# Second block of a two-part network: gate folded into the output weights by GpSimd, norms applied per token out of PSUM, first expert item peeled

## The reference, cut to what matters

```python
h = rms_norm(x, g_mix) * (1.0 + sc1) + sh1
attn = sliding_window_sink_attention(q, k, v, sinks)             # 512 wide
lru  = rg_lru(xc, ...) * gelu(xg)                                # 512 wide
merged = concat([rms_norm(attn, g_attn_out), rms_norm(lru, g_lru_out)])
x = x + gt1 * (merged @ w_out)                                   # gt1: one row of 1024
h = rms_norm(x, g_ffn) * (1.0 + sc2) + sh2
# router: top 4 of 32 experts for each token, softmax over the 4
# expert: gu = h @ w_gu[e] + b_gu[e]; clamp; ((up + 1) * gate * sigmoid(1.702 gate)) @ w_down[e] + b_down[e]
x = x + gt2 * sum of the 4 experts, weighted
return rms_norm(x, g_final)
```

## Time and profile before

| | us |
|---|---|
| median of three runs (2158.57 to 2161.81) | 2161.07 |
| the profiled execution, its own time | 2167.19 |
| its span | 2165.3 |
| TensorE matmul busy | 2047.4 (95%) |
| VectorE / ScalarE / GpSimd busy | 598.2 / 308.1 / 61.6 |
| bytes moved | 598.74 MB, mean 277 GB/s |

### The profile page before, as it was taken

How to read it: one execution, slowest core, us unless ns; L and a number is a source line. 1 busy time by engine, 2 the same in 40 slices (tenths; PEclk the granted TensorE clock), 3 DMA queues, 4 the chain that set the end, 5 groups by cost and what they waited for, 6 DMA issues and landing times.

```text
span 2165.3 us, 24331 instructions
## 1 busy us (share of the span) xinstructions
PE 2047.4 (95%) x10023; PEld 1172.9 (54%) x10023; DVE 598.2 (28%) x1189; ACT 308.1 (14%) x695; POOL 61.6 (3%) x68
## 2 busy tenths in 40 slices
PE   8988999999998999999979999999999999999997
PEld 7766678847866778855735333333333333333332
DVE  0468443312267440003443111111111111111112
ACT  1324210000324310001321000000000000000001
POOL 0022000000012000000001000000000000000000
PEclk9979899999979999999988999999999999999999
DMA  7430068864422036444506999999999999999997
GB/s 301 155 117 1 1 257 301 342 256 156 156 78 79 1 137 228 151 168 155 207 5 272 383 429 427 429 428 429 427 429 428 429 428 428 429 428 429 429 428 298
DMA packets 44272, 598.74 MB, mean 277 GB/s; under 512 B 5056, under 2 KB 5360, under 8 KB 8464
## 3 DMA queue, kind: packets, MB, share of 16 engines
q1 hardware_dynamic: 44208, 597.82, 67.5%
HBM read 596.73 MB, written 1.07 MB: 276 GB/s over the span
## 4 chain that ended last, share of the span: by engine, by line
PE 76%; DMA 16%; DVE 6%; ACT 2%; issue 1%; SPq 0%; DVEq 0%; ACTq 0%
PE ps L1918 16%; DMA ring<-in_stream 16%; PE ps L1240 14%; PE ps L1261 7%; PE ps L1965 7%; PE ps L376 6%; PE ps L1892 3%; PE ps L390 2%; PE ps L1167 2%; PE ps L1907 2%; PE ps L1996 2%; PE ps L1635 2%; PE ps L1474 1%; PE ps L777 1%; PE ps L789 1%
## 5 line engine op out<-in xcount | busy, mean ns | idle before, releaser
L1918 PE MATMUL ps<-ring,HT 128*64 128x512 f32 x2176 | 481.3, 594 | 26.3 <-DMA ring<-in_stream 25.5
L1918 PEld LDWEIGHTS ps<-ring,HT 128*64 128x64 f32 x2176 | 151.9, 137 | 349.2 <-issue 284.8
L1240 PE MATMUL ps<-XT,ring 128*128 128x256 f32 (+1 forms) x1536 | 306.0, 362 | 3.3 <-DVE XT L313 3.3
L1240 PEld LDWEIGHTS ps<-XT,ring 128*128 128x128 f32 x1536 | 271.9, 190 | 36.8 <-DVE XT L313 3.7
L1965 PE MATMUL ps<-SB,HT 128*64 128x512 f32 x1088 | 250.9, 615 | 0.9 <-ACT HT L2021 0.9
L1965 PEld LDWEIGHTS ps<-SB,HT 128*64 128x64 f32 x1088 | 77.4, 141 | 171.6 <-issue 171.6
L1261 PE MATMUL ps<-ring,HT 128*128 128x512 f32 x352 | 151.7, 592 | 0.0
L2069 DVE TENSOR_SCALAR HT<-ps 128x512 f32<-128x512 f32 x34 | 23.5, 692 | 457.2 <-PE ps L1918 457.2
L2013 ACT ACTIVATE HT<-HT 128x512 f32<-128x512 f32 x34 | 21.4, 630 | 781.8 <-DVE HT L2069 781.8
L2081 DVE TENSOR_TENSOR HT<-ps,TOK 128x512 f32<-128x512 f32 x34 | 23.5, 692 | 376.9 <-PE ps L1965 376.9
L376 PE MATMUL ps<-XT,ring 128*128 128x256 f32 x576 | 126.4, 383 | 1.3 <-DMA ring<-in_stream 1.3
(11 more groups left out here) (411 smaller groups left out, 1801.1 us busy)
## 6 DMA issues: line engine op xcount, KB each, us to landing
ring<-in_stream SPq DMA_DIRECT2D x210, 2048.0 KB, 19.7
SB<-in_stream SPq DMA_DIRECT2D x68, 2048.0 KB, 19.8
SB<-in_ln SPq DMA_DIRECT2D x8, 512.0 KB, 9.5
CST<-in_const SPq DMA_DIRECT2D x1, 1362.0 KB, 5.5
PAR<-in_layer SPq DMA_DIRECT2D x2, 558.5 KB, 11.2
X<-in_x SPq DMA_DIRECT2D x1, 1024.0 KB, 5.0
HN<-in_head_norm SPq DMA_DIRECT2D x2, 512.0 KB, 12.0
SB<-mod_rows SPq DMA_DIRECT2D x2, 512.0 KB, 4.4
```

Source lines behind the costliest of these rows:

```text
L1240: m = pe.matmul(ps[:, 2 * (f % 2) + a, j * T + cols.start:j * T + cols.stop], w[:, k, a, j * P:(j + 1) * P], XT[:, k, cols], start=k == 0, ...
L1918: m = pe.matmul(ps[HD * half:HD * (half + 1), a, :], XE[:, 2 * b + k, q * SLOTS_E:(q + 1) * SLOTS_E], w[:, k, a, half, :], start=False, st ...
```

## The change

1. **Gate.** `gated_weights_pool` multiplies the gate row into the two slots of output weights in place, 4 instructions of 128x2048, in GpSimd's list after its layer work and ahead of the rows of the router. The multiplication by `MOD[2]` after the product is gone.
2. **Norms.** The gain of the attention is applied in the copy out of PSUM (`attention_gain_dve`), that of the recurrence in `lru_scan_dve`. The squares of the attention are taken from PSUM. The sum of squares becomes a column for each token tile (products with one column). The products of the two branches go to separate banks, and 1/root is applied per token (per partition) as VectorE adds a bank pair to `X`: `half_residual_dve` for branch 0, `residual_dve` and `residual_half_dve` for branch 1.
3. **Order.** Scores of the last attention unit go ahead of group 7's second half. The products of branch 0 for t = 1 are issued between the last attention units, those for t = 0 behind them. The router multiplies tile 1 in two halves.
4. **Items.** Item 0's down products and item 1's gate and up products come ahead of the loop and of the down biases, with no return of zeros; the loop starts with the stage behind item 1. ScalarE evaluates a Sigmoid on one column before it, and item 0's Sigmoid ahead of the copy of item 1's rows.

The diff, cut to its core:

```diff
+        def attention_gain_dve(v, t):
+            v.wait_ge(S("att_pv"), tiles_before(NU * DEPTH + (4 if t == 0 else 2)))
+            v.wait_ge(S("proj2_ready"), 8)
+            nc.vector.tensor_tensor(OT[:, 0:4, t * P:(t + 1) * P], ps[:, 3 + t, :].rearrange("p (j q) -> p j q", j=4),
+                                    par2("g_attn").unsqueeze(2).broadcast_to([P, 4, P]), ALU.mult).then_inc(S("nsa_out"), 1)
...
         def lru_scan_dve(v, I, L):
-            gelu_out_dve(v, L, DEPTH, HT[:, 4:8, :], GE, GE)
+            x, gated = HT[:, 4:8, :], HT[:, 4:8, :]
+            v.wait_ge(S("tanh"), DEPTH + 1)
+            L(nc.vector.scalar_tensor_tensor(out=GE, in0=GE, scalar=1.0, in1=x, op0=ALU.add, op1=ALU.mult))
+            for c in range(4):
+                (L if c == 3 else I)(nc.vector.tensor_scalar(gated[:, c, :], GE[:, c, :], 0.5, par2("g_lru")[:, c:c + 1], ...))
...
-            nc.vector.tensor_tensor(OT[:, 4:8, :], XC2, GE, ALU.mult).then_inc(S("lru_dve"), 1)
+            nc.vector.tensor_tensor(OT[:, 4:8, :], XC2, gated, ALU.mult).then_inc(S("lru_dve"), 1)
+            nc.vector.scalar_tensor_tensor(out=RA, in0=XC2, scalar=0.5, in1=GE, op0=ALU.mult, op1=ALU.mult).then_inc(S("lru_dve"), 1)
...
+        MIX2_BANK = [{(0, 0): 2, (0, 1): 3, (1, 0): 0, (1, 1): 1}, {(0, 0): 4, (0, 1): 5, (1, 0): 6, (1, 1): 7}]
         def merge_sum_pe(pe, a):
-            for k in ks:
-                m = pe.matmul(ps[:, b, 0:T], cst("ones")[:, 0:P], squares(a)[:, k % 4, :], ...)
+            pe.wait_ge(S("merge_sq"), 2 + a)
+            for t in range(NT):
+                for k in range(4):
+                    m = pe.matmul(ps[:, SS_BANK[a], t:t + 1], (ATT_SQ, RA)[a][:, k, t * P:(t + 1) * P], cst("ones")[:, 0:1], ...)
...
+        def gated_weights_pool(pool):
+            pool.wait_ge(S("mod_rows"), 80)
+            for a in range(2):
+                for c in range(2):
+                    need_slot(pool, AT["wo2", 0, c])
+                    w = slot(AT["wo2", 0, c]).rearrange("p (k n) -> p k n", k=KT)[:, 4 * a:4 * a + 4, :]
+                    nc.gpsimd.tensor_tensor(w, w, MOD[2][:, 512 * c:512 * (c + 1)].unsqueeze(1).broadcast_to([P, 4, 512]), ...
...
         def merge_pe(pe):
+            pe.wait_ge(S("nsa_out"), DEPTH + 2)
+            mix2_pe(pe, 0, 0, 0)
+            pe.wait_ge(S("merge_sq"), 2)
+            mix2_pe(pe, 0, 0, 1)
             merge_sum_pe(pe, 0)
+            pe.wait_ge(S("merge_rms"), 1)
+            pe.wait_ge(S("lru_dve"), 4)
+            mix2_pe(pe, 1, 0, 0)
+            merge_sum_pe(pe, 1)
+            mix2_pe(pe, 1, 0, 1).then_inc(S("mix2_ready"), 1)
+            pe.wait_ge(S("merge_rms"), 2)
+            mix2_pe(pe, 1, 1, 0).then_inc(S("mix2_ready"), 1)
+            transpose_tile_pe(pe, 5, 0, X, ("x_tile", 2 * DEPTH + 1))
+            mix2_pe(pe, 1, 1, 1).then_inc(S("mix2_ready"), 1)
+        def half_residual_dve(v, t, L):
+            L(nc.vector.scalar_tensor_tensor(out=X[:, t, :], in0=bank(MIX2_BANK[0][t, 0], 2), scalar=ROOT[:, t:t + 1],
+                                             in1=X[:, t, :], op0=ALU.mult, op1=ALU.add))
...
         def moe_pe(pe):
             moe_gather_one_pe(pe, 1)
+            moe_turn_rows_pe(pe, 0, 0)
+            moe_turn_hidden_pe(pe, 0, 0)
+            moe_bias_pe(pe, 1, 0)
+            pe.wait_ge(S("moe_ht"), 1)
+            moe_bias_pe(pe, 1, 1)
+            moe_down_pe(pe, 0, 0)
+            pe.wait_ge(S("moe_xe"), 2)
+            moe_gate_up_pe(pe, 0, 1, 1, range(4))
             moe_bias_down_pe(pe)
             with pe.Fori(0, last) as it:
-                moe_between_pe(pe, it, 0)
-                moe_down_pe(pe, it, 0)
-                moe_gate_up_pe(pe, it, 1, 1, range(4))
                 moe_between_pe(pe, it, 1)
                 moe_down_pe(pe, it, 1)
                 moe_gate_up_pe(pe, it, 2, 0, range(4))
+                moe_between_pe(pe, it, 2)
+                moe_down_pe(pe, it, 2)
+                moe_gate_up_pe(pe, it, 3, 1, range(4))
...
         def moe_act(act):
+            moe_gather_one_act(act, 0)
+            nc.scalar.activation(SM[:, 118:119], cst("ln_eps"), ACT.Sigmoid)
+            moe_sigmoid_act(act, 1)
+            moe_gather_one_act(act, 1)
+            moe_turn_act(act, 0, 0)
...
         TensorE's list
+            attention_scores_pe(pe, first + 3)
             project2_pe(pe, 7, 1)
-            attention_scores_pe(pe, first + 3)
             attention_out_pe(pe, first + 1)
-            rg_pe(pe)
-            for n in (first + 2, first + 3):
-                attention_turn_pe(pe, n)
-                attention_out_pe(pe, n)
+            attention_turn_pe(pe, first + 2)
+            rg_pe(pe, range(3))
+            attention_out_pe(pe, first + 2)
+            mix2_pe(pe, 0, 1, 0)
+            attention_turn_pe(pe, first + 3)
+            rg_pe(pe, range(3, 4))
+            attention_out_pe(pe, first + 3)
+            mix2_pe(pe, 0, 1, 1)
             merge_pe(pe)
         ScalarE's list
-            lru_gate_act(act)
-            attention_out_act(act, first + 2)
-            attention_out_act(act, first + 3)
-            lru_decay_act(act, I)
-            merge_square_act(act, 0)
+            attention_out_act(act, first + 3)
+            rg_act(act, 1)
+            attention_square_act(act, 1)
+            lru_decay_act(act, I)
+            lru_gate_act(act)
+            attention_square_act(act, 0)
+            lru_end_act(act)
...
         VectorE's list
             lru_scale_dve(v, L)
-            merge_scale_dve(v, 0, I, L)
             lru_scan_dve(v, I, L)
-            merge_scale_dve(v, 1, I, L)
+            merge_root_dve(v, 0, L)
+            for t in range(NT):
+                half_residual_dve(v, t, L)
+            merge_root_dve(v, 1, L)
+            residual_dve(v, L)
```

More of the change, by code:

```diff
@@ L1499, in program, with rg_act @@
         RG_BANK = (6, 7, 5, 6)
[L1501 to L1507, removed]
+        def rg_act(act, a):
+            to, bias = ((RA, "b_a"), (RI, "b_x"))[a]
+            for c in range(4):
+                if c % 2 == 0:
+                    act.wait_ge(S("rg"), 2 * a + c // 2 + 1)
+                nc.scalar.activation(to[:, c, :], ps[:, RG_BANK[2 * a + c // 2], (c % 2) * T:(c % 2 + 1) * T], ACT.Sigmoid,
+                                     bias=par2(bias)[:, c:c + 1]).then_inc(S("rg_gates"), 1)
         def lru_decay_act(act, I):
@@ L1520, in lru_end_act, with rg_pe @@
             nc.scalar.activation(RA, RA, ACT.Sqrt).then_inc(S("lru_act"), 1)
-        def rg_pe(pe):
+        def rg_pe(pe, pieces):
             pe.wait_ge(S("lru_dve"), 1)
-            pe.wait_ge(S("proj2_evac"), 8)
-            for i in range(4):
+            pe.wait_ge(S("proj2_evac"), 7)
+            for i in pieces:
+                if i == 2:
+                    pe.wait_ge(S("proj2_evac"), 8)
                 if i == 3:
@@ L1618, in merge_scale_dve, with merge_root_dve @@
+        def merge_root_dve(v, a, L):
             v.wait_ge(S("merge_rms"), a + 1)
[L1619 to L1625, removed]
@@ L1628, in mix2_pe @@
         def mix2_pe(pe, a, t, c):
-            ks, b = branch(a)
-            pe.wait_ge(S("merge_scaled"), a + 1)
+            pe.wait_ge(S("wo2_gated"), 2 * a + c + 1)
             need_slot(pe, AT["wo2", 0, c])
             w = slot(AT["wo2", 0, c]).rearrange("p (k n) -> p k n", k=KT)
-            for k in ks:
-                m = pe.matmul(ps[:, MIX2_BANK[t, c], :], OT[:, k, t * P:(t + 1) * P], w[:, k, :],
-                              start=a == 0 and k == ks[0], stop=a == 1 and k == ks[-1], skip_group_check=True)
+            for k in range(4 * a, 4 * a + 4):
+                m = pe.matmul(ps[:, MIX2_BANK[a][t, c], :], OT[:, k, t * P:(t + 1) * P], w[:, k, :],
+                              start=k == 4 * a, stop=k == 4 * a + 3)
@@ L2017, in moe_turn_act @@
             nc.scalar.activation(EPT, ps[:, 3, 0:T], ACT.Copy).then_inc(S("moe_pt"), 1)
-            if q and more:
+            if q == 1 and more:
                 moe_gather_act(act, it * 2 + 3, 0)
@@ L2264, in _ @@
                     inverse_level_pool(pool, l, s)
+            gated_weights_pool(pool)
             for t in range(NT):
```

198 lines of the change are left out of this document (104 added, 94 removed).

## The result

| | before | after |
|---|---|---|
| median, us | 2161.44 (2158.57 to 2165.05, 4 runs) | 2147.69 (2145.12 to 2150.34, 4 runs) |
| ratio | | 0.9936 (0.992 to 0.9952) |
| the profiled execution, its own time | 2167.19 | 2146.03 |

A forecast was written before the change was run, and what follows sets the result against it. Weight transfers bound the items; before their last idle moment, around 1195 us, a latency chain did. Gains 4.3 + 14.9 + 3.8 + 1.2 + 3.5 = 27.7 us took the median from 2161.07 to 2133.4, range 2126 to 2143.

The forecast's parts named there:

- The gate on GpSimd: Gating the output weights: GpSimd finishes before they are needed, covered by the attention; 0 us gained or lost.
- The stretched chain: Rival, merge: GpSimd contention and ScalarE's order bring branch 1's `OT` no earlier; gain 20, 2141 us; chance 0.13.
- The price of the low clock: TensorE at 1.2 GHz: 1.0 us off the merge, up to 4 lost in item 0's down products.
- The dummy products (1.2): Behind the router: `clock_pe` may run at 2.4 GHz, 2.7 us instead of 5.47; gain 0 to 2.7, taken as 1.2.
- The peel (3.5): Item 0 ahead of the loop: down products start 9.2 us earlier, worth 0.5 to 5 at the end, taken as 3.5.
- Merge from `OT` to the last product: Merge, branch 1's `OT` to last output product: 16.7 us instead of 32.6; gain 15.9 less 1.0 for the clock.
- router tail: From last output product to router's counts: about 4.9 us instead of 8.7 through overlapped residual and router products; gain 3.8.
- The frame: Items: transfers' last idle moment, remaining slots at 4.90 us and an unchanged tail set the end; earlier gains kept in full.
- the slower rival: Items' rotated loop: TensorE's pair grows past 58.75 us, each us more costing 16; at 61, 2169 us; chance 0.03.

The follow-up runs named there:

- e4: The kernel before with only the changed kernel's item stage (seven functions of the items' loop): 2158.45 us, ratio 0.9984.
- e1: The changed kernel with GpSimd's gate product cut from 4 instructions of 128x2048 into 16 of 128x512: 2151.13 us, ratio 0.9937.
- e8: The changed kernel with the gate product on VectorE and added dummy products in router and merge: 2131.97 us, ratio 0.9857.
- e11: The changed kernel with GpSimd gating the first output slot, VectorE the second, and added dummy products in router and merge: 2132.10 us, ratio 0.9868.
- e12: A repeat of e8, the same kernel once more: 2134.0 us, ratio 0.987.
- e5: The changed kernel with the gate product moved from GpSimd to VectorE, at places where it waits: 2140.32 us, ratio 0.989.
- e6: The changed kernel with 4 instead of 3 dummy products behind the router's counts and a wider one behind the second sum: 2146.18 us, ratio 0.9914.
- e10: The changed kernel, gate product still on GpSimd, with added dummy products in both merge and router: 2145.47 us, ratio 0.9915.
- e9: The changed kernel with GpSimd gating only the first output slot's two pieces and VectorE the second slot's: 2138.28 us, ratio 0.9894.

## Why the prediction was wrong

The sum was 27.7 us; the landmark moved by 202.3 - 188.6 = 13.7. Step by step, each difference from the table:

- **"The gate on GpSimd (0)" failed**, by 8.1 us. I asked only whether GpSimd would be done in time (it was: 1053.76, with need at 1080) and not whom it holds meanwhile. My sentence was "the cover is the attention"; but VectorE's small instructions, on which the attention waits, were the ones that were held. The trace that I had cited held the answer. L754's 2.27 us beside 1.28 alone I read as two engines sharing a bandwidth, and made of it only a price for GpSimd. Beside it, in the trace of before, stood this row of VectorE:

```profile
182.41 1.23 DVE L1147 TENSOR_TENSOR SA<-SA,SM 128x1024 f32<-128x1024 f32 x1
```

  GpSimd's instruction is noted as started at 182.50, VectorE's ends at 183.64, and 1.28 us from there is 184.92; the end noted is 184.77. To about 0.15 us that is an instruction that waits for the other's end and then runs at its full pace, not one that runs slowly. The Trainium skill, "Advanced Engine Details and Errata", section VectorE Performance Modes, says that VectorE's second SBUF port is shared with GpSimd, "so GPSIMD instructions and 2p Vector instructions will interfere/block eachother". It says this of instructions in a mode with two read ports, and no run here shows the mode of the instructions that were held. Of its two words, block is the one that the rows of the changed kernel and of e1 bear out.
- *The stretched chain*, the rival at 0.13 that gave 2141, was of the right kind and too small. It had `OT` come no earlier than before and 8 us lost in all; `OT` came 3.8 later than before, 8.1 lost there alone, and the clock's loss came on top.
- **The price of the low clock** was put in the wrong places. For branch 1's first products 1.0 was set, and it was 2.8 (6.45 against 3.67): 1.8 short. The rest was placed in item 0's down products, which took 7.09 as before. It fell instead on the gather, the biases and the first slot, which I had left at their rows of before: 7.4 us. With the 8.1 of the first step and the 1.8 these make 17.3; 0.7 came back at the router's tail and 2.7 in the peel.
- **The dummy products (1.2)**: right in size. 2.65 shorter, and 1.2 of it was left at the start of the gather (6.5 us behind them instead of 7.8). That the same step would leave the gather at the low clock I did not see.
- **The peel (3.5)**: the mechanism held in each part. The issue behind item 0's down products came 9.8 us earlier against the first ring load (9.2 predicted), and a second, shorter hole opened one load later. The size was low: 0.6 more at the first part, 2.1 at the second, so 6.2. Of the 2.1, 1.3 had been set aside for a low clock; it didn't come in this execution's return (1.99), but it did in e4's (3.68), so that much of the 6.2 is luck.
- **Merge from `OT` to the last product, router tail**: 13.1 gained where 14.9 were predicted (the clock again), and 4.5 where 3.8 were.
- **The frame** held: the end is the landmark plus 940.5 to 941.2 us, and nothing was lost in TensorE's loop, so the slower rival was wrong.
- With the three causes removed (e8), the sum comes out near the predicted one: `OT` 77.5 (78.0), last product's end 94.3 (95.7), landmark 174.1 (174.6), and a median of 2132 to 2134, with 2133 forecast. The profiled executions of e11 and e12 give the same landmark (174.1, 174.4). That speaks against a further large cause. The close match is in part luck: the 2.6 us that are still lost behind the router are made up by gains elsewhere, and e8 has dummy products that the forecast kernel had not.

**Open.** Which stretch of TensorE gets the low clock is shown for each run and not explained: e5, e6 and e10 each still hold a slow first slot (5.35 to 6.35), in e9 and in the kernel before it is 3.65. e11, which joins e9's front with the dummies, is no better than e8. e9's profiled execution is the fastest of its six (2134.94, median 2138.28), so its landmarks flatter it. That TENSOR_SCALAR from SBUF is held too rests on five rows (L1124 1.51 and L1827 1.24 in the changed kernel; L1124 0.80, L1127 1.31 and L1541 2.50 in e1), against 0.16 to 0.17 for the small ones and 0.73 for L1541 undisturbed.

## What to carry to other kernels

Here work on GpSimd was free where VectorE waited or ran products with an input in PSUM and a reduction (e9), and being off the critical path was not enough. Look at what VectorE runs in the same microseconds. As the upper end of the price take the time from the first instruction that is held to the end of GpSimd's work: 10.4 us here, of which 6.9 reached the first transposition. Don't expect smaller pieces to lower it. If a step makes TensorE's work shorter or moves it, price the next wide products behind it at both clock levels, not only those behind the wait that you have in view.

## What the runs showed of the hardware

- GpSimd and VectorE kept each other waiting for whole instructions. VectorE's 128x4 from two SBUF inputs took 4.43 us beside GpSimd's 128x2048 (4.5) and 1.18 beside its 128x512 (1.28), against 0.16 alone. A reduction (1.22) and products with one input in PSUM (0.68) kept their length. GpSimd's 128x512 took 2.27 instead of 1.28 when it began beside VectorE's 128x1024 of 1.23.
- The elementwise product of 128x2048 in fp32 took 2.2 to 2.3 us on VectorE and 4.5 on GpSimd.
- TensorE was granted 1.2 GHz for 14.6 us in which it was busy throughout, with the gather's products of 64 columns at first and those of 512 behind them (6.16 for the slot instead of 3.65). One dummy product of 512 columns more ahead of it, and another widened from 256 to 512 (e6), brought the gather to 3.75, but not the slot behind it (5.35).
- TensorE got the low clock with no wait ahead of it: in e6 it was busy throughout from 1185.8 to 1199.0 and was granted 1.00, then 0.52 from 1189.5 to 1193.0, then 1.00.
- Executions of kernels that are the same up to there differed by 12 us in when the second block begins (1010.7 to 1023.0 over 14 runs), and e8 and e12, the same kernel, by 3.2.
